# Two of x's four loads on ScalarE's queue, and four small re-orderings, in a fused two-block fp32 kernel

## The reference

```python
def first_block(x, c, ctx, c_ctx, ...):
    sh1, sc1, gt1, sh2, sc2, gt2 = split(silu(c) @ w_ada + b_ada, 6)      # the same for c_ctx
    pl = project(modulate(rmsnorm(x, g_mix), sh1, sc1), w_in, ...)         # q, k, v, g, decays, conv, gates
    pc = project(modulate(rmsnorm(ctx, g_mix), sh1c, sc1c), w_in, ...)
    _, s_f, s_b = gla_bidir(pc...)                       # linear-attention heads on the context: states
    o, _, _ = gla_bidir(pl..., s_f, s_b)                 # and on x, from these states
    x = x + gt1 * merge_branches(o, g, conv..., gates...)
    x = x + gt2 * swiglu(modulate(rmsnorm(x, g_ffn), sh2, sc2), ...)
    return rmsnorm(x, g_final)

def second_block(h, ...):                                # two layers
    # layer 0: conv + pooling mixer, swiglu;  layer 1: hgrn2 mixer (8 gated heads), swiglu
    #   hgrn2: f = lb + (1-lb)*sigmoid(f_raw); k = 1-f; chunks of 64 tokens; scores within a chunk
    #   are sums over pairs (t, s) of q_t k_s exp(b_t - b_s); state S carried from chunk to chunk
    return rmsnorm_2(h, final_g)
```

## Time and profile before

| what | value |
|---|---|
| median of 3 runs | 2099.54 us |
| profiled execution, its own time | 2100.01 us |
| its span (first to last instruction) | 2098.2 us |
| TensorE busy | 2073.4 us, 99% of the span |
| VectorE, ScalarE, GpSimd busy | 1596.8, 1024.8, 793.3 us |
| mean granted TensorE clock | 0.997 of full speed |

### The profile page before, as it was taken

The page is one execution under the profiler, slowest core; times in us unless marked ns, Lnnn a source line. Parts: engine busy times, 40 slices in busy tenths (PEclk is TensorE's granted clock), DMA queues, the critical chain, the costliest instruction groups (busy, mean ns, idle before and its releaser), DMA issues.

```text
span 2098.2 us, 33961 instructions
## 1 busy us (share of the span) xinstructions
PE 2073.4 (99%) x12839; PEld 1808.9 (86%) x12839; DVE 1596.8 (76%) x2411; ACT 1024.8 (49%) x1727; POOL 793.3 (38%) x496
## 2 busy tenths in 40 slices
PE   8999999999999999999999999999999999999997
PEld 6888888889988999997878999998888878999996
DVE  3766556776469877768977899885788877888985
ACT  3515655644454444445564444444666754444433
POOL 2332444255431433334854333333333334233332
PEclk9999999999999999999999999999999999999999
DMA  8571222122423322332032222322222123233231
GB/s 319 208 263 61 81 81 71 56 96 97 162 84 101 111 91 100 112 111 95 31 109 101 91 92 97 115 91 91 81 82 80 60 71 111 71 111 101 91 119 52
DMA packets 60126, 217.61 MB, mean 104 GB/s; under 512 B 6736, under 2 KB 7888, under 8 KB 58832
## 3 DMA queue, kind: packets, MB, share of 16 engines
q1 hardware_dynamic: 59984, 215.68, 30.4%
HBM read 213.55 MB, written 2.10 MB: 103 GB/s over the span
## 4 chain that ended last, share of the span: by engine, by line
PE 90%; DVE 5%; ACT 2%; issue 2%; DMA 0%; DVEq 0%; POOL 0%; ACTq 0%; SPq 0%
PE ps L789 12%; PE ps L791 12%; PE ps L790 12%; PE ps L1312 8%; PE ps L1311 8%; PE ps L1310 8%; PE ps L1325 5%; PE ps L1326 5%; PE ps L1327 5%; PE ps L1195 1%; PE ps L1194 1%; PE ps L1193 1%; PE ps L1018 1%; PE ps L1019 1%; PE ps L1020 1%
## 5 line engine op out<-in xcount | busy, mean ns | idle before, releaser
L554 POOL TENSOR_TENSOR w_lo<-w_raw,w_hi 128x1024 fp32r<-128x1024 f32 (+1 forms) x169 | 409.6, 2443 | 529.8 <-ACT w_hi L1696 524.8
L789 PE MATMUL ps<-h_hi,w_lo 128*128 128x512 f32 x896 | 355.9, 397 | 2.2 <-DVE h_lo L2416 0.9
L791 PE MATMUL ps<-h_hi,w_hi 128*128 128x512 f32 x896 | 349.6, 390 | 0.0
L790 PE MATMUL ps<-h_lo,w_hi 128*128 128x512 f32 x896 | 349.6, 390 | 0.0
L1696 ACT ACTIVATE w_hi<-w_raw 128x1024 fp32r<-128x1024 f32 (+1 forms) x176 | 177.9, 1036 | 128.0 <-PE ps L791 71.1
L1310 PE MATMUL ps<-ht_hi,w_lo 128*128 128x256 f32 x816 | 231.0, 283 | 0.2 <-DVE x L2819 0.2
L1311 PE MATMUL ps<-ht_lo,w_hi 128*128 128x256 f32 x816 | 230.9, 283 | 0.0
L1312 PE MATMUL ps<-ht_hi,w_hi 128*128 128x256 f32 x816 | 230.9, 283 | 0.0
L789 PEld LDWEIGHTS ps<-h_hi,w_lo 128*128 128x128 f32 x896 | 168.4, 188 | 40.3 <-issue 4.0
L791 PEld LDWEIGHTS ps<-h_hi,w_hi 128*128 128x128 f32 x896 | 168.4, 188 | 35.9
L605 POOL TENSOR_TENSOR w_lo<-w_raw,w_hi 128x512 fp32r<-128x512 f32 x51 | 66.1, 1296 | 352.4 <-ACT p_five L2184 299.5
(11 more groups left out here) (538 smaller groups left out, 5104.0 us busy)
## 6 DMA issues: line engine op xcount, KB each, us to landing
w_raw<-in_w_ffn_in SPq DMA_DIRECT2D x132, 512.0 KB, 3.8
out_raw<-in_w_ffn_out SPq DMA_DIRECT2D x57, 512.0 KB, 5.8
w_raw<-in_w_hg SPq DMA_DIRECT2D x40, 512.0 KB, 4.1
ada_w<-in_w_ada SPq DMA_DIRECT2D x32, 512.0 KB, 5.6
w_raw<-in_w_conv_gate SPq DMA_DIRECT2D x32, 512.0 KB, 4.2
w_raw<-in_w_merge SPq DMA_DIRECT2D x32, 512.0 KB, 4.1
w_raw<-in_w_cp SPq DMA_DIRECT2D x20, 512.0 KB, 3.8
w_raw<-in_w_qkv SPq DMA_DIRECT2D x16, 512.0 KB, 6.3
```

Source lines behind the costliest of these rows:

```text
L554: pool.tensor_tensor(w_lo[s][:, 0:n], raw[s][:, 0:n], w_hi[s][:, 0:n].bitcast(F32), ALU.subtract).then_inc(lo_done[s], 1)
L789: pe.matmul(out, wl, hi, start=first, stop=False)
L790: pe.matmul(out, wh, lo, start=False, stop=False)
L791: return pe.matmul(out, wh, hi, start=False, stop=last)
```

## The change

Nothing that is computed changes. The parts:

1. SP issues x's parts 0 and 2 first, then `cond_col` and `vec`; ScalarE issues parts 1 and 3 on its own queue before anything else.
2. ScalarE loads the Ln table (by a Ln of one element) before the squares, not after them; TensorE does 4 products for the clock instead of 8 before `mod_sums(0)`.
3. `w_lo` of unit 2 is made by VectorE in two halves instead of GpSimd; ScalarE converts units 2 and 3 one row group earlier. TensorE does unit 2's pairs with groups 0 and 1 before `mod_turn(3)`, and unit 3's with groups 0 to 2 before `mod_turn(4)`.
4. k_v(0) goes to bank 7 and k_v(1) to bank 6, and the wait for `scores_read` moves from k_v(0) to k_v(1).
5. `act_hi` of slot 2 in `act_gated` at j = 3 instead of 4.
6. Last gated head: banks of its levels (0, 1, 4, ...), keys through bank 1 and values through bank 4, ScalarE copies the values, levels 2 to 6 in one row, and `begin(1)` asks for one level less to be read.

```diff
@@ sp_start
-            sp.dma_start(cond_col[:, :, :], dram["cond_cols"]).then_inc(S["small_in"], 16)
-            for i in range(4):
+            for i in (0, 2):
                 sp.dma_start(x_all[:, 2 * i:2 * i + 2, 0:T], ...).then_inc(S[f"x_in{i}"], 16)
+            sp.dma_start(cond_col[:, :, :], dram["cond_cols"]).then_inc(S["small_in"], 16)
@@ act_start
+            for i in (1, 3):
+                act.dma_start(x_all[:, 2 * i:2 * i + 2, 0:T], ...).then_inc(S[f"x_in{i}"], 16)
             act.wait_ge(S["small_in"], 16)
...
+            act.wait_ge(S["const_step"], 3)
+            act.activation(spare[:, 8:9], ones[:, 0:1], ACT.Ln)
...
-            act.activation(spare[:, 8:9], ones[:, 0:1], ACT.Ln)
...
-                if k == 0:
-                    act_hi(act, 1, 0)
-                if k in (2, 3):
-                    act_hi(act, k, 0)
+                if k < 3:
+                    act_hi(act, k + 1, 0)
@@ pool_first
-            for s in (0, 2, 3):
+            for s in (0, 3):
@@ pe_start
-                keep_clock(2 if i < 3 else 8)
+                keep_clock(2 if i < 3 else 4)
...
-            pairs(stage(2)[:2])
+            pairs(stage(2)[2:4])
             mod_turn(3)
-            pairs(stage(2)[2:])
+            pairs(stage(2)[:2] + stage(2)[4:])
             mod_sums(4)
-            pairs(stage(3)[:1])
+            pairs(stage(3)[3:6])
             mod_turn(4)
-            pairs(stage(3)[1:])
+            pairs(stage(3)[:3] + stage(3)[6:])
@@ dve_start
             unit_low(1, 1).then_inc(lo_done[1], 1)
+            unit_low(2, 0)
             modulation(2)
             value(2)
+            unit_low(2, 1).then_inc(lo_done[2], 1)
             low(2)
@@ pe_gla, k_v
                             pe.wait_ge(S["kd_low"], 2 * w + 1)
+                        if n == 1:
                             pe.wait_ge(S["scores_read"], w + 1)
...
-                        out = ps[:, (6, 7, 0, 2)[n % 4], 0:HEAD_V]
+                        out = ps[:, (7, 6, 0, 2)[n % 4], 0:HEAD_V]
@@ act_gated
-                if j == 4:
+                if j == 3:
                     act_hi(act, side_slot(2), side_q(2))
@@ pe_hg, the end
-            keys(7)
-            values(7, 1, 1)
+            keys(7, 1)
+            values(7, 1, 4)
...
-            score(2)
+            for l in range(2, 7):
+                score(l)
             output(3, 5, 6)
-            for l in range(3, 7):
-                score(l)
-            begin(1, 7 * 7 + 6)
+            begin(1, 7 * 7 + 5)
@@ act_hg, dve_hg
-            decays(7, 1, between=lambda: key_rows(7))
+            decays(7, 1, lambda: key_rows(7, 1), lambda: value_rows(7, 4))
-            decays(7, 1, lambda: value_rows(7, 1))
+            decays(7, 1)
```

More of the change, by code:

```diff
@@ L43 @@
 SCORE_BANKS = (7, 0, 1, 2, 3, 5, 4)
-SCORE_BANKS_LAST = (0, 4, 1, 0, 4, 1, 0)
+SCORE_BANKS_LAST = (0, 1, 4, 0, 1, 4, 0)
 ROUNDS = FC // 2
@@ L409, in sp_start @@
         def sp_start(sp):
+            for i in (0, 2):
+                sp.dma_start(x_all[:, 2 * i:2 * i + 2, 0:T], dram["x"][:, 2 * i:2 * i + 2, :]).then_inc(S[f"x_in{i}"], 16)
             sp.dma_start(cond_col[:, :, :], dram["cond_cols"]).then_inc(S["small_in"], 16)
-            for i in range(4):
-                sp.dma_start(x_all[:, 2 * i:2 * i + 2, 0:T], dram["x"][:, 2 * i:2 * i + 2, :]).then_inc(S[f"x_in{i}"], 16)
             sp.dma_start(vec[:, :], dram["vectors"]).then_inc(S["vec_in"], 16)
@@ L1537, in turn_back, with keys @@
                 mm.then_inc(S["hoT_mm"], 1)
-            def keys(g):
+            def keys(g, bank=4):
                 pe.wait_ge(S["hkd_ready"], g + 1)
                 for c in range(TT):
-                    mm = pe.transpose(ps[:, 4, c * P:(c + 1) * P], hkd[:, c * P:(c + 1) * P], ident[:, :])
+                    mm = pe.transpose(ps[:, bank, c * P:(c + 1) * P], hkd[:, c * P:(c + 1) * P], ident[:, :])
                 mm.then_inc(S["hkd_mm"], 1)
@@ L1719, in act_start @@
         def act_start(act):
+            for i in (1, 3):
+                act.dma_start(x_all[:, 2 * i:2 * i + 2, 0:T], dram["x"][:, 2 * i:2 * i + 2, :]).then_inc(S[f"x_in{i}"], 16)
             act.wait_ge(S["small_in"], 16)
@@ L2275, in log, with decays @@
                 act.activation(hlf[:, :], hlf[:, :], ACT.Ln).then_inc(S["hlog_ready"], 1)
-            def decays(g, par, between=None):
+            def decays(g, par, between=None, ahead_of_last=None):
                 act.wait_ge(S["hd_ready"], 7 * g + 1)
@@ L2284, in decays @@
                         between()
+                    if i == 5 and ahead_of_last:
+                        ahead_of_last()
                     act.wait_ge(S["hd_ready"], 7 * g + i + 2)
@@ L2313, in high, with key_rows, value_rows @@
                 act.activation(at_index(r_hi, g), ps[:, 4, :], ACT.Copy).then_inc(S["r_hi"], 1)
-            def key_rows(g):
+            def key_rows(g, bank=4):
                 act.wait_ge(S["hkd_mm"], g + 1)
                 wait_former(act, S["hkv_mm"], 7 * g)
-                act.activation(hkd_tok[:, :, :].rearrange("p c k -> p (c k)"), ps[:, 4, :], ACT.Copy)\
+                act.activation(hkd_tok[:, :, :].rearrange("p c k -> p (c k)"), ps[:, bank, :], ACT.Copy)\
                    .then_inc(S["hkd_tok_ready"], 1)
+            def value_rows(g, bank):
+                act.wait_ge(S["hv_mm"], g + 1)
+                act.wait_ge(S["ho_mm"], g)
+                act.activation(hv_tok[:, :, :].rearrange("p c k -> p (c k)"), ps[:, bank, :], ACT.Copy)\
+                   .then_inc(S["hv_tok_ready"], 1)
             def root(g, bank=5):
@@ L2423, in dve_start, with unit_low @@
             dve.wait_ge(S["norm_rstd"], 2)
-            def second_low(part):
+            def unit_low(s, part):
                 n = slice(part * (D // 2), (part + 1) * (D // 2))
-                dve.wait_ge(hi_done[1], 1)
-                return dve.tensor_tensor(w_lo[1][:, n], raw[1][:, n], w_hi[1][:, n].bitcast(F32), ALU.subtract)
+                dve.wait_ge(hi_done[s], 1)
+                return dve.tensor_tensor(w_lo[s][:, n], raw[s][:, n], w_hi[s][:, n].bitcast(F32), ALU.subtract)
             value(0)
@@ L2434, in dve_start @@
             value(1)
-            second_low(0)
+            unit_low(1, 0)
             low(1)
             turn_in(2)
-            second_low(1).then_inc(lo_done[1], 1)
+            unit_low(1, 1).then_inc(lo_done[1], 1)
+            unit_low(2, 0)
             modulation(2)
             value(2)
+            unit_low(2, 1).then_inc(lo_done[2], 1)
             low(2)
@@ L2644, in head @@
                         n = m - 1
-                        kv = ps[:, (6, 7, 0, 2)[n % 4], 0:HEAD_V]
+                        kv = ps[:, (7, 6, 0, 2)[n % 4], 0:HEAD_V]
                         dve.wait_ge(S["kv_mm"], 5 * w + m)
```

## The result

The changed kernel takes 2103.93 us (median of 22 runs, 2102.05 to 2106.41), the kernel before, in 22 runs beside it, 2099.72 (2098.4 to 2104.6). The ratio is 1.0019, 95% interval 1.0013 to 1.0025: slower by 4 us, where 2100.6 was forecast with a range up to 2103.3. The profiled execution took 2103.77 us, 3.8 more than that of before.

The account below looks back on a forecast made before the run. TensorE, busy 2073.4 us or 99% of the span, was taken as the bound. Terms +3.6 +1.7 -1.3 -2.1 +0 -0.8 = +1.1 on 2100.01 give 2101.1, as a median 2100.6 us; range 2094.0 to 2103.3.

Parts of the forecast that it names:

- The term for that clock, +1.7: Start: after its idle time TensorE runs at half pace for some 3.4 us, losing 1.7 us (0 to 2.3).
- to the end whole: From about 33 us on TensorE has next to no idle time, so any first-stage shift reaches the end in full.
- step L = 9.0: Start: the conditions' load, queued behind two parts of x, lands at 9.0 us (range 8 to 9.9).
- L + 3.6 to the first sum, 5.8 us of work behind: Start: TensorE's first sum of squares starts 3.6 us after the conditions land; then 5.8 us of work until mod_sums(0).
- rival (c): Start: TensorE stays at 1.2 GHz until mod_sums(0), losing 5.8 us instead of 1.7; +5.2 in all, 2104.7 us; chance 8%.
- (a): Start: conditions late, but TensorE's clock doesn't fall or recovers in under a microsecond; -0.6 in all, 2098.9 us; chance 20%.
- (b): Start: the conditions don't queue behind x and land before 5 us; -5.2 in all, 2094.3 us; chance 22%.
- Pairs -1.3: First stage: re-ordered pairs and VectorE's w_lo remove TensorE's waits for row group 2 and unit 2; -1.3 us (0.7 to 1.6).
- Linear heads -2.1: Linear heads: k_v(0) no longer waits for the scores' read; 1.3 us in head 0, 0.8 in the others (0.8 to 2.2).
- Merge copy 0: Merge: the earlier act_hi leaves TensorE's 1.3 us wait for y_out unchanged; 0 us (-0.4 to +0.4).
- Last gated head -0.8: Last gated head: TensorE's 0.62 us wait goes and the rest moves up with VectorE; -0.8 us (0 to -1.3).

Follow-up runs that it names:

- e1: Changed kernel with the conditions' load first on SP's queue again, x still split over two queues: 2099.95 us, ratio 1.0002 to the kernel before.
- e4: Changed kernel with 34 instead of 10 small products at TensorE's start, over the wait for the conditions: 2100.46 us, ratio 1.0002 to the kernel before.
- e12: Changed kernel with the linear heads' banks and wait for the scores as before: 2108.65 us (4 runs), ratio 1.0042 to the kernel before.
- e13: Changed kernel with the first stage's pairs and w_lo of unit 2 as before: 2103.00 us, ratio 1.0017 to the kernel before.
- e9: Kernel before with the first stage's pairs edit (with unit 2's w_lo on VectorE) alone: 2099.49 us, ratio 0.9995 to the kernel before.
- e2: Kernel before with the changed order and queues of x's and the conditions' loads alone: 2104.96 us, ratio 1.0024 to the kernel before.
- e6: Kernel before with the last gated head's edits alone: 2098.24 us, ratio 0.9996 to the kernel before.
- e5: Changed kernel with x's and the conditions' loads as before, all on SP's queue, conditions first: 2097.14 us, ratio 0.9989 to the kernel before.
- e10: Kernel before with the edits of the linear heads and of the last gated head: 2096.42 us, ratio 0.9984 to the kernel before.
- e14: Kernel before with the edits of the linear heads, merge copy and last gated head: 2096.01 us, ratio 0.9982 to the kernel before.
- e11: Kernel before with the pairs edit and the last gated head's edits: 2098.98 us, ratio 0.9995 to the kernel before.
- e3: Changed kernel with the loads, the Ln table load's place and the 8 products for the clock as before: 2096.83 us, ratio 0.9989 to the kernel before.

## Why the prediction was wrong

The mechanism at the start was right: the conditions queue behind x, ScalarE holds the squares back, TensorE idles and its clock falls. Two steps failed. The term for that clock, +1.7, was too small: it measured 3.0. And the step that lets the shift of the first stage pass "to the end whole" put all of TensorE's time behind it at nothing: 2.8 us arose there. Of these only some 0.5, part 3's, are tied to an edit; for the rest the cause stays open.

- **Landing of the conditions** (step L = 9.0): right, 9.25 in the first profile, and 8.9 to 9.4 in the five others with this order of loads. The Trainium skill's rule ("DMA: Bandwidth & Descriptors", "Queues, rings and completion order"), rings served in turn and each in order, gave 9.5: the trace agrees to within 0.1 to 0.6 us. Its section "Issuing engines are not separate DMA queues" adds that a second issuing engine saves only issue time; e1 agrees, and shows a cost beside: the first part lands later.
- **L + 3.6 to the first sum, 5.8 us of work behind**: right: 12.82 is 3.57 behind 9.25, and e4 shows the 5.8 (12.46 to 18.39 is 5.9).
- **The clock, +1.7: this term was mis-sized.** 3.0 in the profile, 1.9 in the second; 2.4 and 2.6 in e12 and e13, whose start is the same. I had taken the 3.4 us of half pace after tenths of idle time; after 5.8 us idle half pace lasted to 18.3, 5.5 us. All but the 1.9 lie above the 2.3 that the prediction gave as the upper bound; rival (c), 5.8, was too high: the clock recovered before mod_sums(0). Rivals (a) and (b) are out: the clock fell, the conditions queued.
- **Pairs -1.3**: right at their place, in the changed kernel and in e9 alone; the price of 0.5 in the gated-head loop was missed. **Linear heads -2.1**: 2.5, outside the range of 0.8 to 2.2; the 0.27 in heads 1 to 3 was 0.34, and 1.52 in head 0, more than the 1.3 of the earlier trace rows, as a tail was probably hidden behind it. **Merge copy 0**: right. **Last gated head -0.8**: 0.9, and e6 alone too.
- **"A shift of the first stage passes to the end whole"**: right as to the shift (e2), but the sum had no term for TensorE's clock elsewhere. The late dip (+1.7), the idle time of L1573 (+0.7) and the loop's +0.4 (part 3's price) are 2.8 us that the sum lacks; the start, +1.4 (clock and landing), is about made up for by the missing early dip (-0.8) and the heads (-0.4), which is luck.
- How much of the 4 us between the medians is the late dip can't be said: only profiles show it, two of the changed kernel's. The mean granted clock, which is on record for every run, says that dips differ from run to run: of the changed kernel's 22 runs, the eight from 2102.05 to 2102.55 us have 0.996 to 0.997, the seven from 2105.56 to 2106.41 us have 0.994 to 0.995. Firm are e2 (+5 us for part 1 alone), and e5 against the changed kernel: 0.9989 against 1.0019, 6.3 us for the same part with the others in place.

Parts 4 and 6 do what they say: e10 and e14, without any edit to the first stage, beat both kernels, the kernel before by 0.16% and 0.18%. Part 5 brings nothing that can be told. Part 2 was not run alone. Part 3 nets 0.8 us in the profiles, and the runs don't show even that: of four pairs of kernels that differ in it alone, the one with it has the lower ratio in two (e9 against the kernel before, 0.9995 and 1; e11 against e6, 0.9995 and 0.9996) and the higher in two (e3 against e14, 0.9989 and 0.9982; the changed kernel against e13, 1.0019 and 1.0017), all within their intervals.

## What to carry to other kernels

Put the small load that starts an engine's in-order program first on its queue; behind megabytes it lands when they do. When an edit makes the matrix engine wait for microseconds, price the wait and the half pace after it, which cost 1.9 to 3.0 us here after waits of 2.2 to 6.1 us, or fill the wait with products: in e4 that brought mod_sums(0) forward by 3.1 us. Before a lost microsecond late in a profile is put down to an edit, profile the same kernel twice and look at the spread of its runs.

## What the runs showed that I had not expected

- The 8 KB load: 1.7 us on a free queue, 2.3 with x on two queues behind it, 7.1 to 7.6 behind two parts of x, in six profiles.
- Two queues on x: first part in use at 6.99 instead of 5.28, last squares done at 11.46 instead of 11.12.
- Half pace costs much the same after waits of different length: 1.9 us after 2.2 us of idle time (e1), 2.1 after 4.0 (e2), 1.9 and 3.0 after 5.8 to 6.1 in two executions of the changed kernel. With products over the wait it is at most 0.3 in the sums. After 1.7 to 1.8 us of idle time late in the kernel: 1.7 lost in some executions, nothing in others.
- Re-ordering pairs in the first 40 us makes TensorE wait 0.5 us longer some 1550 us later, in every one of 11 profiles.
- The granted clock can read 1.00 over a stretch whose products run at half pace, where the trace has no record of it (10 to 18.5 us of the changed kernel); in the profiles of e12 and e13, whose first sums took 2.08 too, the same stretch reads 0.66.
- TensorE idle for 0.7 to 1.5 us in a run of seven short products, 14 records (L1573), in the first turn of the gated-head loop, in 8 of 20 profiles, with no semaphore event at its end.
